# Norm chains with pre-added squares, one root table, and three output tiles abreast behind a norm

## The chip, the cores and the metric

The kernel runs on one core of one Trainium2 chip. The metric is device time in microseconds of one execution, as the median of several.

## The reference

Two layers of a diffusion backbone over 512 tokens (256 context, 256 latent), model width 1024, all in float32. What matters here:

```
def rmsnorm(x, g):
    y = xf * lax.rsqrt(jnp.mean(xf * xf, axis=-1, keepdims=True) + NORM_EPS)
    return y * g

for l in range(DEPTH):
    h  = modulate(rmsnorm(x, norm_mix_pre[l]), mod[0], mod[1])      # norm 0
    z  = h @ w_in[l]                                                # 24 tiles of 128 outputs
    ys = four mixers over z (short convolution, neighbourhood attention, GQA, RWKV-7)
    m  = merge_branches(h, ys, w_branch[l], w_gate[l], b_gate[l], w_o[l])
    x  = x + mod[2] * rmsnorm(m, norm_mix_post[l])                  # norm 1
    f  = conv_ffn(modulate(rmsnorm(x, norm_ffn_pre[l]), mod[3], mod[4]), ...)   # norm 2
    x  = x + mod[5] * rmsnorm(f, norm_ffn_post[l])                  # norm 3

def conv_ffn(h, w_up, w_conv, w_down):
    u = dwconv3(h @ w_up, w_conv)
    return (u[..., :D_FF] * jax.nn.silu(u[..., D_FF:])) @ w_down
```

In the second layer only the latent half is needed after the mixers, so most tiles there are 256 columns wide instead of 512.

## The kernel before

Features lie on partitions (1024 features are KT = 8 slices of 128), tokens on columns. Each weight column block of 128 outputs ("half" of a ring slot) gives one output tile. Matmuls of the projections are done in three products: ScalarE copies a weight half from `ring` to `whi` (rounded, L751), VectorE subtracts to get `wlo` (L1076), and `project` (L1502 to L1504) adds high by high, high by low and low by high for each of the 8 slices into one PSUM bank. There are SPLIT = 3 slots of `whi`/`wlo`; a slot is refilled when the tile that used it is done (`split_until`, on both engines). The ring has three slots of 1 MB, loaded by SyncE's queue (L577) in a fixed order; a slot is reloaded when both its halves are split, or for the modulation weights when TensorE has used it.

A norm goes through four engines. ScalarE squares each slice (`square`, L724); TensorE adds the squares over partitions and slices with eight matmuls against ones (`sum_squares`, L1483, full float32, two passes each); ScalarE makes the root as exp(-0.5 ln(mean + eps)) (`norm_root`, L730 and L733), each of the two functions behind a table load; VectorE multiplies. Norms 1 and 3 end in `residual` (L1137, L1143): slice by slice into X. Norms 0 and 2 end in a modulated input: VectorE times the root (L1129), ScalarE scale and shift (L779) and rounded copy (L785), VectorE the low part (L1115), one slice after the other, each counted in `h_ready`; the next projection waits slice by slice in its first tile alone (`made`).

Norm 1 reads the out-projection (`wo`), whose 8 tiles are copied to OB (L1012) and squared from there. Norm 3 does so with the down projection (F, L1051). Norm 3 also needs X back from DRAM: GpSimd's queue issues that load (L707) when the last down tile is done, because the feed-forward's hidden values lie over X. Then it issues the small bias tables of the next layer. At the end of layer 0 TensorE also makes three blocks of modulation values (L1518, L1525), from ring slots that the first z weights wait for.

In the up projection the bank of a tile is copied by ScalarE with a convolution factor (L1039), VectorE adds the two neighbours (L1440, L1442), in program order ahead of the next low half for the same pair of tiles. In the z projection banks are only copied.

Every engine executes its own program in order; semaphores join them. The order of TensorE's jobs is a list (`JOB`), each job takes the next of 8 banks.

Of the kernel before, what the change touches and what calls it, by code (L numbers as in the profile page):

```python
# [17 lines left out]
ALU = mybir.AluOpType  # L18
# [6 lines left out]
KT = DM // P  # L25
# [7 lines left out]
FT = DFF // P  # L33
# [48 lines left out]

STRIP = 32
STRIPS = P // STRIP
RING = 3
SLOT_N = 256
SPLIT = 3
NBANK = 8


# [184 lines left out]
def half_no(job):  # L275

    return HALF[blocks_of(job)[0]]


def build(nc, a, out):  # L280
    ctx = ExitStack()
    with ctx:
# [3 lines left out]
        def sem(name):  # L286
            return ctx.enter_context(nc.semaphore(name))
# [163 lines left out]
        u_lo = sem("u_lo")  # L451
        setup = sem("setup")
        sq_ready = sem("sq_ready")
        h_full = sem("h_full")
        scaled = sem("scaled")
        h_half = sem("h_half")
# [45 lines left out]
        def frees(name):  # L502

            return bank_free[JOB[name] % NBANK]

        def emptied(eng, name):

            eng.wait_ge(frees(name), JOB[name] // NBANK + 1)

# [10 lines left out]
        def norm_no(l, k):  # L520
            return 4 * l + k
# [193 lines left out]
        def _(act):  # L715
# [7 lines left out]
            def square(dst, src):  # L723
                act.activation(dst, src, ACT.Square).then_inc(sq_ready, 1)  # L724
# [73 lines left out]
            for l in range(LAYERS):  # L798
# [188 lines left out]
                for J in range(4):  # L987
# [17 lines left out]
                    for j in (2 * J, 2 * J + 1):  # L1005
                        act.wait_ge(gated, added(l, j, 3))
                        act.activation(AR[:, 0, j, c0:c1], ACC[:, j, c0:c1], ACT.Copy).then_inc(acc_hi, 1)

                for j in range(KT):
                    s = filled(act, ("wo", l, j))  # L1010
                    split_until(min(half_no(("wo", l, j)) + 1 + SPLIT, half_no(("up", l, 0, 0)) + SPLIT))
                    act.activation(OB[:, j, c0:c1], s[:, c0:c1], ACT.Copy).then_inc(frees(("wo", l, j)), 1)  # L1012
                    emptied(act, ("wo", l, j))
                    square(SQB[:, j, c0:c1], OB[:, j, c0:c1])
                norm_root(l, 1)
                for i in range(KT):
                    act.wait_ge(x_ready, 16 * l + i + 1)
# [10 lines left out]
                for j in range(FT):  # L1028
# [14 lines left out]
                    emptied(act, ("up", l, j, 1))  # L1043
                    act.activation(dst, dst, ACT.Silu).then_inc(silu_done, 1)
                product_hi(FT - 1)
                for j in range(KT):
                    split_until(half_no(("down", l, j)) + (5 if j < KT - 1 else 3))
                    s = filled(act, ("down", l, j))
                    if j < KT - 1:
                        split_until(half_no(("down", l, j)) + 6)  # L1050
                    act.activation(F[:, j, c0:c1], s[:, c0:c1], ACT.Copy).then_inc(frees(("down", l, j)), 1)  # L1051
                    emptied(act, ("down", l, j))
                    square(SQF[:, j, c0:c1], F[:, j, c0:c1])
                norm_root(l, 3)
                fill(("end", l, 0))

# [2 lines left out]
        def _(dve):  # L1059
# [95 lines left out]
            for l in range(LAYERS):  # L1155
# [243 lines left out]
                for J in range(4):  # L1399
                    for i in range(4):  # L1400
                        for j in (2 * J, 2 * J + 1):
                            split_until(min(half_no(("gate", l, j, i)) + SPLIT, half_no(("wo", l, 0)) + SPLIT))
                            no = 8 * J + 2 * i + (j - 2 * J)
                            gt = (rt, rs)[no % 2][:, c0:c1]
                            s = filled(dve, ("br", l, j, i))[:, c0:c1]
                            emptied(dve, ("gate", l, j, i))
                            o = ACC[:, j, c0:c1]
                            dst = o if i == 0 else gt
                            dve.tensor_tensor(dst, gt, s, ALU.mult).then_inc(frees(("br", l, j, i)), 1)  # L1409
                            emptied(dve, ("br", l, j, i))  # L1410
                            if i:
                                dve.tensor_tensor(o, o, gt, ALU.add).then_inc(gated, 1)
                        if READOUT.get((J, i)) == "g2":
                            readout()
                    for j in (2 * J, 2 * J + 1):
                        dve.wait_ge(acc_hi, 8 * l + j + 1)
                        dve.tensor_tensor(AR[:, 1, j, c0:c1], ACC[:, j, c0:c1], AR[:, 0, j, c0:c1].bitcast(F32),
                                          ALU.subtract).then_inc(acc_lo, 1)
                for j in range(KT):
                    split_until(min(half_no(("wo", l, j)) + 1 + SPLIT, half_no(("up", l, 0, 0)) + SPLIT))  # L1420

                gains(l, (1, 2, 3))
# [21 lines left out]
                    if j:  # L1444
                        product_lo(j - 1)
                product_lo(FT - 1)
                split_until(half_no(("down", l, 0)) + 3 * KT)
                for j in range(KT):
                    emptied(dve, ("down", l, j))
                dve.wait_ge(x_back, 32 * (l + 1))  # L1450
# [6 lines left out]
        def _(pe):  # L1457
# [10 lines left out]
            def done(ins):  # L1468
                count[0] += 1
                ins.then_inc(mm_done, 1)  # L1470
# [7 lines left out]
            def sum_squares(l, k, src):  # L1478
                c0, c1 = cols(l) if k else (0, T)
                o = job(("ss", l, k))  # L1480
                for i in range(KT):
                    pe.wait_ge(sq_ready, 8 * norm_no(l, k) + i + 1)
                    last = pe.matmul(o[:, c0:c1], K("ones"), src[:, i, c0:c1], start=(i == 0), stop=(i == KT - 1))  # L1483
                done(last)
# [8 lines left out]
            def project(name, part, c0, c1, kn=KT, made=None):  # L1493
# [14 lines left out]
                        last.then_inc(w_used, 1)  # L1508
                done(last)

            def fill(point):
                for name in FILL.get(point, []):
                    if name[0] == "mod":
                        w = weights(("ada",) + name[1:])
                        o = job(name)
                        for k in range(KT):
                            g = k % STRIPS
                            last = pe.matmul(o[STRIP * g:STRIP * g + STRIP, 0:SLOT_N], cpad[:, k, :], w[:, k, :],  # L1518
                                             start=(k < STRIPS), stop=(k >= KT - STRIPS))
                    else:  # L1520
                        pe.wait_ge(const_in, 16)
                        emptied(pe, ("mod",) + name[1:])
                        o = job(name)
                        for x in range(2):
                            last = pe.matmul(o[:, 2 * x:2 * x + 2], mrow[:, P * x:P * x + P], K("fold", 2),  # L1525
                                             start=True, stop=True)
                    done(last)

            pe.wait_ge(silu_c, 1)
            for l in range(LAYERS):  # L1530
                c0, c1 = cols(l)
                fill(("start", l, 0))
                sum_squares(l, 0, YB)
                fill(("start", l, 1))
                for n, t in enumerate(Z_ORDER):
                    z0, z1 = cols(l, t)
                    project(("z", l, t), lambda x, k: HR[:, x, k, z0:z1], z0, z1,
                            made=None if n else (h_ready, 16 * l))
                    if n == 5:
                        for i in range(3):  # L1540
                            q0, q1 = cols(l, Z_GQ + i)
# [285 lines left out]
                sum_squares(l, 1, SQB)  # L1827
                sum_squares(l, 2, SQB)

                for j in range(FT):  # L1830
                    for g in range(2):
                        project(("up", l, j, g), lambda x, k: H2[:, x, k, c0:c1], c0, c1,
                                made=None if j or g else (h_ready, 16 * l + 8))
                for j in range(KT):
                    project(("down", l, j), lambda x, k: hidden(x, k)[:, c0:c1], c0, c1, FT,
                            made=None if j else (u_lo, FT * l))
# [49 lines left out]
```

## Time and profile before

| | before |
|---|---|
| median of 3 runs | 2061.64 us (2061.12 to 2065.96) |
| the profiled execution | 2068.02 us, span 2066.2 us |
| TensorE busy | 1911.5 us, 93% |
| VectorE busy | 985.8 us, 48% |
| ScalarE busy | 821.6 us, 40% |
| GpSimd busy | 284.1 us, 14% |
| granted TensorE clock, mean | 0.962 |
| table loads on L730 and L733 | 8 and 8, 1283 ns each |

The span is the time from the first to the last instruction of one profiled execution; busy is the time in which an engine executed. An instruction's row names kernel line, engine, operation and tiles, out<-in. The clock is the share of TensorE's full clock (2.4 GHz) that was granted. Matmuls overlap, so their starts are compared, not their durations.

### The profile page before, as it was taken

Reading aid. Unit: us, or ns where it says so; the run is one execution under the profiler, and the core shown is the slowest. Engines: PE = TensorE matmul, PEld = TensorE weight load, DVE = VectorE, ACT = ScalarE, POOL = GpSimd, SP = SyncE. Lnnn points to the kernel's source line nnn. Section 1 sums busy time; section 2 is a strip of 40 time slices with the busy share of each in tenths; the row PEclk is TensorE's granted clock in tenths of the full one; section 3 lists DMA queues with packets and bytes.
Section 4 is the critical chain, followed back from the end, with each engine's and each line's share of the span. In section 5 each row is a group of like instructions: output and inputs, shape, how many; then the busy total and the mean of one; then the engine's idle time right before and its main releaser. Section 6 shows DMA issues by size and latency. Waiting matters only on the chain. (4 is left out here: it accounts for less than half of the span.)

```text
span 2066.2 us, 27988 instructions
## 1 busy us (share of the span) xinstructions
PE 1911.5 (93%) x11608; PEld 1571.5 (76%) x11608; DVE 985.8 (48%) x1555; ACT 821.6 (40%) x1306; POOL 284.1 (14%) x227
## 2 busy tenths in 40 slices
PE   4899998989999999799999996999897999989997
PEld 1688557959877777478888883875695989979997
DVE  1353437456333333455554215544646535557763
ACT  2421455152232223543433225325515234366653
POOL 1040432021000000011121001304202000002211
PEclk9899999989999999899999997999898999989999
DMA  8632642020342322223232336533101045444654
GB/s 243 212 101 82 194 145 82 1 76 7 88 157 82 102 68 96 82 67 117 82 102 78 96 112 174 188 119 119 62 1 62 1 133 166 159 135 150 198 160 126
DMA packets 225646, 228.64 MB, mean 111 GB/s; under 512 B 5169, under 2 KB 214321, under 8 KB 225393
## 3 DMA queue, kind: packets, MB, share of 16 engines
q1 hardware_dynamic: 210560, 190.40, 29.2%
q0 software_dynamic: 14960, 36.44, 6.1%
q8 instruction: 94, 1.54, 0.3%
q14 instruction: 32, 0.25, 0.0%
HBM read 214.24 MB, written 12.58 MB: 110 GB/s over the span
## 5 line engine op out<-in xcount | busy, mean ns | idle before, releaser
L751 ACT ACTIVATE whi<-ring 128x1024 fp32r<-128x1024 f32 (+1 forms) x264 | 275.4, 1046 | 688.4 <-PE ps L1504 624.8
L1076 DVE TENSOR_TENSOR wlo<-ring,whi 128x1024 fp32r<-128x1024 f32 (+1 forms) x264 | 319.4, 1213 | 212.8 <-ACT whi L751 212.1
L1502 PE MATMUL ps<-H,whi 128*128 128x512 f32 (+1 forms) x704 | 241.0, 342 | 13.1 <-DVE H L1115 13.0
L1503 PE MATMUL ps<-H,whi 128*128 128x512 f32 (+1 forms) x704 | 238.9, 339 | 0.0
L1504 PE MATMUL ps<-H,wlo 128*128 128x512 f32 (+1 forms) x704 | 238.7, 339 | 0.0
L1502 PE MATMUL ps<-HG,whi 128*128 128x512 f32 (+1 forms) x512 | 181.3, 354 | 0.1
L1504 PE MATMUL ps<-HG,wlo 128*128 128x512 f32 (+1 forms) x512 | 172.1, 336 | 0.0
L1503 PE MATMUL ps<-HG,whi 128*128 128x512 f32 (+1 forms) x512 | 172.1, 336 | 0.0
L1502 PE MATMUL ps<-HR,whi 128*128 128x512 f32 (+1 forms) x384 | 144.3, 376 | 23.1 <-DVE HR L1115 23.1
L1502 PEld LDWEIGHTS ps<-H,whi 128*128 128x128 f32 x704 | 134.7, 191 | 32.0 <-issue 13.4
L1504 PEld LDWEIGHTS ps<-H,wlo 128*128 128x128 f32 x704 | 135.1, 192 | 13.8
L1503 PEld LDWEIGHTS ps<-H,whi 128*128 128x128 f32 x704 | 135.2, 192 | 13.5
L1503 PE MATMUL ps<-HR,whi 128*128 128x512 f32 (+1 forms) x384 | 140.9, 367 | 0.0
L1504 PE MATMUL ps<-HR,wlo 128*128 128x512 f32 (+1 forms) x384 | 140.8, 367 | 0.0
L1502 PEld LDWEIGHTS ps<-HG,whi 128*128 128x128 f32 x512 | 97.1, 190 | 14.3 <-issue 4.5
L1502 PE MATMUL ps<-UA,whi 128*128 128x512 f32 (+1 forms) x320 | 107.5, 336 | 0.0
L1503 PE MATMUL ps<-UA,whi 128*128 128x512 f32 (+1 forms) x320 | 107.5, 336 | 0.0
L1504 PE MATMUL ps<-UA,wlo 128*128 128x512 f32 (+1 forms) x320 | 107.5, 336 | 0.0
L1503 PEld LDWEIGHTS ps<-HG,whi 128*128 128x128 f32 x512 | 97.1, 190 | 13.6 <-issue 3.8
L1504 PEld LDWEIGHTS ps<-HG,wlo 128*128 128x128 f32 x512 | 97.1, 190 | 10.1
L1502 PEld LDWEIGHTS ps<-HR,whi 128*128 128x128 f32 x384 | 74.6, 194 | 39.4 <-issue 19.5
L1409 DVE TENSOR_TENSOR rt<-rt,ps 128x512 f32<-128x512 f32 (+1 forms) x24 | 13.3, 554 | 160.1 <-PE ps L1809 152.8
(285 smaller groups left out, 3619.1 us busy)
## 6 DMA issues: line engine op xcount, KB each, us to landing
ring<-in_ada_w SPq DMA_DIRECT2D x48, 1024.0 KB, 5.3
ring<-in_ffn_up SPq DMA_DIRECT2D x44, 1024.0 KB, 5.1
ring<-in_w_gate SPq DMA_DIRECT2D x32, 1024.0 KB, 5.5
ring<-in_w_in SPq DMA_DIRECT2D x24, 1024.0 KB, 5.2
ring<-in_ffn_down SPq DMA_DIRECT2D x32, 512.0 KB, 3.9
WB<-in_w_branch POOLq DMA_DIRECT2D x8, 1024.0 KB, 7.3
ring<-in_w_o SPq DMA_DIRECT2D x8, 1024.0 KB, 5.3
ring<-in_ffn_down SPq DMA_DIRECT2D x16, 384.0 KB, 3.5
```

The costliest lines, as they stand in the source:

```text
L751: act.activation(whi[:, m % SPLIT, 0:kn, :], ring[:, SLOT[raw] % RING, 0:kn, P * half:P * half + P], ACT.Copy).then_inc(hi_done, 1)
L1076: dve.tensor_tensor(wlo[:, m % SPLIT, 0:kn, :], ring[:, SLOT[raw] % RING, 0:kn, P * half:P * half + P], whi[:, m % SPLIT, 0:kn, :].bitcast ...
L1409: dve.tensor_tensor(dst, gt, s, ALU.mult).then_inc(frees(("br", l, j, i)), 1)
L1502: pe.matmul(o[:, c0:c1], hi[:, i, :], part(0, k), start=(k == 0), stop=False)
L1503: pe.matmul(o[:, c0:c1], hi[:, i, :], part(1, k), start=False, stop=False)
L1504: last = pe.matmul(o[:, c0:c1], lo[:, i, :], part(0, k), start=False, stop=(k == kn - 1))
```

## The change

Four edits:

- Squares of norms 1 and 3 are taken from the PSUM bank ahead of the copy. VectorE adds squares 1 to 6 to square 0 as they come (`sum_square`), in the loops over `wo` and `down`; `sum_squares` then makes two matmuls, over slice 0 (the sum of seven) and slice 7. For norms 0 and 2 it keeps its eight.
- The last weight half behind the out-projection is split after the square and the copy instead of before.
- `preload_act_table_set("natural_log_exp_and_others")` stands ahead of the `wo` loop and of the `down` loop.
- `project_first` replaces `project` for the first three tiles of z and of up: slices 0 to 4 go through all three tiles, then each tile takes its last three slices.

```diff
+ROOT_TABLE = "natural_log_exp_and_others"
+ABREAST = 5
...
+                act.preload_act_table_set(ROOT_TABLE)
                 for j in range(KT):
                     s = filled(act, ("wo", l, j))
-                    split_until(min(half_no(("wo", l, j)) + 1 + SPLIT, half_no(("up", l, 0, 0)) + SPLIT))
+                    if j < KT - 1:
+                        split_until(min(half_no(("wo", l, j)) + 1 + SPLIT, half_no(("up", l, 0, 0)) + SPLIT))
+                    square(SQB[:, j, c0:c1], s[:, c0:c1])
                     act.activation(OB[:, j, c0:c1], s[:, c0:c1], ACT.Copy).then_inc(frees(("wo", l, j)), 1)
-                    emptied(act, ("wo", l, j))
-                    square(SQB[:, j, c0:c1], OB[:, j, c0:c1])
+                split_until(half_no(("up", l, 0, 0)) + SPLIT)
                 norm_root(l, 1)
...
+                act.preload_act_table_set(ROOT_TABLE)
                 for j in range(KT):
                     split_until(half_no(("down", l, j)) + (5 if j < KT - 1 else 3))
                     s = filled(act, ("down", l, j))
                     if j < KT - 1:
                         split_until(half_no(("down", l, j)) + 6)
+                    square(SQF[:, j, c0:c1], s[:, c0:c1])
                     act.activation(F[:, j, c0:c1], s[:, c0:c1], ACT.Copy).then_inc(frees(("down", l, j)), 1)
-                    emptied(act, ("down", l, j))
-                    square(SQF[:, j, c0:c1], F[:, j, c0:c1])
                 norm_root(l, 3)
...
+                def sum_square(k, SQ, j):
+                    n = 2 * l + k // 2
+                    dve.wait_ge(sq_ready, 8 * norm_no(l, k) + j + 1)
+                    if j > 1:
+                        dve.wait_ge(sq_summed, (KT - 2) * n + j - 1)
+                    dve.tensor_tensor(SQ[:, 0, c0:c1], SQ[:, 0, c0:c1], SQ[:, j, c0:c1], ALU.add).then_inc(sq_summed, 1)
                 for j in range(KT):
+                    if 1 < j:
+                        sum_square(1, SQB, j - 1)
                     split_until(min(half_no(("wo", l, j)) + 1 + SPLIT, half_no(("up", l, 0, 0)) + SPLIT))
...
-                split_until(half_no(("down", l, 0)) + 3 * KT)
+                for j in range(KT):
+                    split_until(half_no(("down", l, 0)) + min(3 * j + 6, 3 * KT))
+                    if 0 < j < KT - 1:
+                        sum_square(3, SQF, j)
...
             def sum_squares(l, k, src):
-                for i in range(KT):
+                if k % 2:
+                    pe.wait_ge(sq_summed, (KT - 2) * (2 * l + k // 2 + 1))
+                for i in (0, KT - 1) if k % 2 else range(KT):
                     pe.wait_ge(sq_ready, 8 * norm_no(l, k) + i + 1)
                     last = pe.matmul(o[:, c0:c1], K("ones"), src[:, i, c0:c1], start=(i == 0), stop=(i == KT - 1))
...
+            def project_first(names, part, cs, made):
+                outs = [job(name, n) for n, name in enumerate(names)]
+                tiles = []
+                for name in names:
+                    tiles += halves(name)
+                order = [(k, n) for k in range(ABREAST) for n in range(len(names))]
+                order += [(k, n) for n in range(len(names)) for k in range(ABREAST, KT)]
+                for k, n in order:
+                    c0, c1 = cs[n]
+                    o, (hi, lo) = outs[n][:, c0:c1], tiles[n]
+                    if n == 0:
+                        pe.wait_ge(made[0], made[1] + k + 1)
+                    pe.matmul(o, hi[:, k, :], part(0, k)[:, c0:c1], start=(k == 0), stop=False)
+                    pe.matmul(o, hi[:, k, :], part(1, k)[:, c0:c1], start=False, stop=False)
+                    last = pe.matmul(o, lo[:, k, :], part(0, k)[:, c0:c1], start=False, stop=(k == KT - 1))
+                    if k == KT - 1:
+                        done(last)
...
+                project_first([("z", l, t) for t in Z_ORDER[:SPLIT]], lambda x, k: HR[:, x, k, :],
+                              [cols(l, t) for t in Z_ORDER[:SPLIT]], (h_ready, 16 * l))
...
+                ups = [("up", l, j, g) for j in range(FT) for g in range(2)]
+                project_first(ups[:SPLIT], lambda x, k: H2[:, x, k, :], [(c0, c1)] * SPLIT, (h_ready, 16 * l + 8))
+                for name in ups[SPLIT:]:
+                    project(name, lambda x, k: H2[:, x, k, c0:c1], c0, c1)
```

## Rows read from the trace of the kernel before

**Rows 1.** Timeline, all engines, layer 0, norm 1: start us, duration, instruction, [idle <-releaser]
```profile
843.56 7.03 PE L1483 MATMUL ps<-SQB,con 128*128 128x512 f32 x16
843.84 1.06 ACT L751 ACTIVATE whi<-ring 128x1024 fp32r<-128x1024 f32 x1 [3.23 <-PE ps L1504]
...
845.41 0.63 ACT L724 ACTIVATE SQB<-OB 128x512 f32<-128x512 f32 x1
...
846.26 0.17 DVE L1102 TENSOR_TENSOR amod<-mod,vec 128x16 f32<-128x16 f32 x1
...
851.33 1.28 ACT L733 ACT_TABLE_LOAD   x1
...
853.39 1.29 DVE L1137 TENSOR_TENSOR OB<-OB,rs 128x512 f32<-128x512 f32 x2 [6.96 <-ACT rs L733]
```

**Rows 2.** The same timeline at norm 2 of layer 0
```profile
866.60 0.69 ACT L730 ACTIVATE rt<-ps,eps 128x512 f32<-128x512 f32 x1
```

**Rows 3.** Timeline, layer 0, up projection: first tile, second tile, fourth weight's low half
```profile
873.58 0.77 PE L1502 MATMUL ps<-H,whi 128*128 128x512 f32 x1 [7.05 <-DVE H L1115]
...
884.02 0.39 PE L1502 MATMUL ps<-H,whi 128*128 128x512 f32 x1
```
```profile
887.42 1.22 DVE L1076 TENSOR_TENSOR wlo<-ring,whi 128x1024 fp32r<-128x1024 f32 x1
```

**Rows 4.** Timeline, layer 0, z projection: first matmul of the first and fourth tile
```profile
66.99 0.76 PE L1502 MATMUL ps<-HR,whi 128*128 128x512 f32 x1 [5.28 <-DVE HR L1115]
```
```profile
88.11 0.39 PE L1502 MATMUL ps<-HR,whi 128*128 128x512 f32 x1
```

**Rows 5.** Timeline from the last down tile of layer 0 to norm 0 of layer 1
```profile
1238.11 0.92 POOL L707 DMA_DIRECT2D X<-xsave  x1 [114.83 <-PE ps L1504]
...
1245.73 60.31 SPq L577 DMA_DIRECT2D ring<-in_w_in  x7
...
1248.01 1.29 DVE L1137 TENSOR_TENSOR F<-F,rs 128x512 f32<-128x512 f32 x2 [23.21 <-DMA X<-xsave]
...
1259.29 0.63 ACT L724 ACTIVATE YB<-X 128x512 f32<-128x512 f32 x1 [0.16 <-DVE X L1143]
...
1269.84 1.90 DVE L1129 TENSOR_TENSOR Z<-X,rs 128x512 f32<-128x512 f32 x3 [2.71 <-ACT rs L733]
```

**Rows 6.** Timeline, TensorE, layer 1, z projection
```profile
1274.09 0.55 PE L1502 MATMUL ps<-HR,whi 128*128 128x256 f32 x1 [12.93 <-DVE HR L1115]
...
1284.49 0.41 PE L1502 MATMUL ps<-HR,whi 128*128 128x256 f32 x1
...
1288.91 0.28 PE L1502 MATMUL ps<-HR,whi 128*128 128x256 f32 x1
...
1294.74 0.39 PE L1502 MATMUL ps<-HR,whi 128*128 128x512 f32 x1
```

**Rows 7.** Timeline, layer 1, norm 1 and the up projection
```profile
1835.37 1.06 ACT L751 ACTIVATE whi<-ring 128x1024 fp32r<-128x1024 f32 x1 [1.10 <-PE ps L1504]
```
```profile
1841.08 0.76 DVE L1137 TENSOR_TENSOR OB<-OB,rs 128x256 f32<-128x256 f32 x2 [3.11 <-ACT rs L733]
...
1863.49 1.22 DVE L1076 TENSOR_TENSOR wlo<-ring,whi 128x1024 fp32r<-128x1024 f32 x1
```
```profile
1854.24 0.55 PE L1502 MATMUL ps<-H,whi 128*128 128x256 f32 x1 [4.86 <-DVE H L1115]
...
1860.80 0.41 PE L1502 MATMUL ps<-H,whi 128*128 128x256 f32 x1
...
1867.21 0.28 PE L1502 MATMUL ps<-H,whi 128*128 128x256 f32 x1
```

**Rows 8.** Timeline, VectorE, norm 3 of layer 1
```profile
2055.58 0.76 DVE L1137 TENSOR_TENSOR F<-F,rs 128x256 f32<-128x256 f32 x2 [12.39 <-DMA X<-xsave]
```

**Rows 9.** Windows: busy time of each engine, granted clock, DMA share, GB/s
```profile
66.90:70.20 3.30, 3.21 (x7) 2.15 (x8) 1.39 (x2) 3.30 (x8) 0.00 (x0) 0.50 0.83 292
```
```profile
1606.00:1650.00 44.00, 44.00 (x387) 43.69 (x386) 28.85 (x43) 9.57 (x18) 0.00 (x0) 1.00 0.01 1
```

More of the change, by code:

```diff
@@ L453, in build @@
         sq_ready = sem("sq_ready")
+        sq_summed = sem("sq_summed")
         h_full = sem("h_full")
@@ L1534, in _ @@
                 fill(("start", l, 1))
+                project_first([("z", l, t) for t in Z_ORDER[:SPLIT]], lambda x, k: HR[:, x, k, :],
+                              [cols(l, t) for t in Z_ORDER[:SPLIT]], (h_ready, 16 * l))
                 for n, t in enumerate(Z_ORDER):
                     z0, z1 = cols(l, t)
-                    project(("z", l, t), lambda x, k: HR[:, x, k, z0:z1], z0, z1,
-                            made=None if n else (h_ready, 16 * l))
+                    if n >= SPLIT:
+                        project(("z", l, t), lambda x, k: HR[:, x, k, z0:z1], z0, z1)
                     if n == 5:
@@ L1828, in _ @@
                 sum_squares(l, 2, SQB)
[L1830 to L1833, printed above, removed]
+                ups = [("up", l, j, g) for j in range(FT) for g in range(2)]
+                project_first(ups[:SPLIT], lambda x, k: H2[:, x, k, :], [(c0, c1)] * SPLIT, (h_ready, 16 * l + 8))
+                for name in ups[SPLIT:]:
+                    project(name, lambda x, k: H2[:, x, k, c0:c1], c0, c1)
                 for j in range(KT):
```

## The prediction

> **What bounds the kernel now.** TensorE is busy for 93% of the span, so the first question is where it waits. I read the timeline at the places where a norm feeds a projection. The first matmul of each such projection carries its wait: 7.05 us before the up projection of layer 0 [rows 3], 12.93 us before the z projection of layer 1 [rows 6], 4.86 us before the up projection of layer 1 [rows 7]. In front of these waits TensorE sums squares at the pace of other engines. Then the timeline of all engines through one norm [rows 1] gives the chain inside. Then the timeline at the end of each layer, where a norm root has a rival for the latest arrival, the reload of X [rows 5, 8]. Everything else in the projections is paced by TensorE and the change leaves it so.
>
> I call three matmuls of one slice (high by high, high by low, low by high) a triple, and the eight triples of a tile its work. In layer 1's z projection seven triples at 256 columns took 1288.91 - 1284.49 = 4.42 us, or 0.64 each, with matmuls of 0.41 us; from 1288.91 the same matmul lasts 0.28, and one narrow triple with the eight at 512 columns behind it took 1294.74 - 1288.91 = 5.83 us [rows 6], which is 0.36 + 8 x 0.68. The granted clock has two levels: 0.50 (1.2 GHz) in a stretch of layer 0's z, 1.00 (2.4 GHz) in the mixing stage [rows 9], and the step at 1288.9 is that between them. So a triple takes 0.36 and 0.68 us at full clock for the two widths, 0.64 and, twice that, 1.28 at half.
>
> **Norm 1, layer 0.** Before, ScalarE sees the last out-projection tile at 843.84, splits a weight half (1.06), copies the bank, squares (0.63), and waits: TensorE needs 7.03 us for the eight column sums, which begin at 843.56 and end at 850.6. Then logarithm (0.69, [rows 2]), table load 1.28, exponential, and the residual starts at 853.39 [rows 1]. After, six of the eight sums are made on VectorE. Each is an addition of 128x512, which I price by the two multiplications of that shape, 1.29 us [rows 1]; VectorE has one 1.22 us split [rows 3] in each tile of the out-projection (8 x 0.68 = 5.4 us), so the six lie hidden. In layer 1 they cost about 0.4 each beside 1.2 in 2.9 us; hidden too. Without that cover they would cost 6 x 0.65 = 3.9 us in layer 0. TensorE does two sums: the first at once, the second when the last square is there (844.5), 7.03 / 8 = 0.88 us, ready at 845.5. ScalarE now does square 0.6, copy 0.6, split 1.06, to 846.1, then logarithm 0.7 and exponential 0.6 with no load: root at 847.4. What is late next is VectorE: its low half of the split starts when ScalarE has split, and the gain products follow. Before, the last of these ended at 846.43, 1.5 us after the split's 844.90 [rows 1]; after, 846.1 + 1.5 = 847.6, and with the semaphores between some 847.9. Gain 853.39 - 847.9 = 5.5 us.
>
> **Norm 2, layer 0.** The first load hides already: squares end, TensorE still sums, the logarithm starts at 866.60 without a wait behind its load [rows 2], one 1.28 us load after a last square that needed about as long on TensorE. Only the second load goes: 1.3 us.
>
> **The price of a load.** In the rows a load lasts 1.28 us, from 851.33 to 852.61, and the residual starts at 853.39 [rows 1]; of the 0.78 us between, some 0.63 are the exponential (the square of that shape takes as long). The Trainium skill, ScalarE: Activation LUTs, section What ACT_TABLE_LOAD costs, gives 1.28 us for the load and 1.38 us for a drain beside it; with six exposed loads gone (below) the sum would be 6 x 1.38 = 8.3 us better by it. The trace disagrees: 0.15 us are left for a drain.
>
> **Norm 1 and 2, layer 1.** The same with 256 columns: from 1835.37 square 0.4, copy 0.4, split 1.06, then 1.5 to the end of the gains and 0.2 for semaphores, so 1838.9 instead of 1841.08 [rows 7]: 2.2 us. Norm 2: 1.3 us.
>
> **Norm 3, both layers: nothing.** The residual waits for X, not for the root: in layer 0 VectorE's wait of 23.21 us ends with the DMA of X at 1248.01, issued when the last down tile was done, 1238.11 [rows 5]; in layer 1 the same, 12.39 us to 2055.58 [rows 8]. The shorter chain ends earlier behind a transfer that doesn't move. The load put ahead of the down loop costs 1.28 us of ScalarE, while TensorE has a split half in hand. I price it at nothing; uncovered it would be 1.3 us a layer.
>
> **Norm 0 of layer 1: where a collision starts.** Before: X lands at 1247.9, last square at 1259.9, a wait for weights, three splits, load, logarithm, load, exponential, and the first product at 1269.84 [rows 5]. After, both loads go (norm 3 left the right table, and only squares and copies run between). But TensorE is free 5 us sooner after the last down tile, its modulation matmuls release ring slots, and the first w_in load, issued at 1245.73 [rows 5], is issued near 1240.7: inside the 9.7 us of the X load. If they share the rate, X lands about 3 us later, 1251. From X's landing: 12.0 to the last square (as before), three splits 3.1, logarithm and exponential 1.3: X + 16.5 = 1267.8 against 1269.84. Gain 2.0 us. If X isn't delayed, 5.4; if it lands at 1256, a loss of 2.7.
>
> **Three tiles abreast.** The first tile of z in layer 1 took 1284.49 - 1274.09 = 10.4 us for eight slices of the normed input [rows 6], so a slice of 512 columns comes about every 1.5 us (the last two come closer), and one triple takes 0.68. After, each slice up to the fifth feeds three triples, 2.0 us, so TensorE doesn't wait for input once it has begun. The work is the same, so what counts is when the third tile ends, and the clock.
> z, layer 0: from 66.99 to 88.11, where the fourth begins, 21.1 us [rows 4]. The window 66.9 to 70.2 has clock 0.50 [rows 9]. After: 3.3 us at half clock (2.6 triples), 21.4 triples x 0.68 = 14.6, so 17.9. Gain 3.2, rounded with the start to 3.3.
> up, layer 0: the first tile from 873.58 to 884.02 [rows 3], two more of 5.45, 21.3 us. After: 5.4 us at half clock (as in z of layer 1, below; 4.2 triples) plus 19.8 x 0.68 = 18.9. Then a new wait. All three split slots are held until the first tile ends, which is now two threes of triples (4.1 us) ahead of the third's end, not two tiles. Before, from that tile's end (884.02) the low half of the fourth weight started at 887.42 and took 1.22: 4.6 us [rows 3], behind a bank evacuation and two convolution steps. So a wait of 0.6 us. Gain 2.4 - 0.6 = 1.8.
> z, layer 1: 1274.09 to 1294.74, 20.65 us, at half clock to 1288.9 [rows 6]. After: tiles of 256, 256 and 512 columns, a slice is 2.56 us at half clock and 1.40 at full. 5.4 us at half clock (an estimate: the second tile starts without a gap at 1284.49 and the step comes 4.4 us later [rows 6], with a triple or two ahead of it), the rest of five slices to 9.45, then 0.36 x 3 + 0.36 x 3 + 0.68 x 3: 13.65. Gain 7.0. The fourth weight is late by nothing: z has no convolution before its split.
> up, layer 1: 1854.24 to 1867.21, 12.97 us [rows 7]. After, the three tiles would end at 11.0, but the fourth weight comes 3.9 us after the first tile's end (before 1860.80 to 1863.49 plus 1.22), that is at 8.9 + 3.9 = 12.8. Gain 0.1; between -0.9 and 1.1 with the clock's rise at 7.9 or 3.3 us.
> Sum: norms 5.5 + 1.3 + 2.2 + 1.3 + 2.0 = 12.3; abreast 3.3 + 1.8 + 7.0 + 0.1 = 12.2; together 24.5 us.
>
> The profiled execution took 2068.02 us with a span of 2066.2, so I expect a span near 2041.7; its time is 6.4 us over the median of 2061.64. I take the 24.5 from the median: **2037 us**, 1.2% less.
>
> **The rivals.**
> 1. The clock stays low while three banks alternate. The Trainium skill, TensorE: Matmul & The Clock Gate, section A second HAM failure mode: psum-queue depth-cycling, says that cycling through banks lets the clock fall back. As a mechanism of this kernel: z and up of layer 0 wholly at half clock, 24 x 1.28 = 30.7 us instead of 21.1 and 21.3; z of layer 1 20.5, even; up of layer 1 24 x 0.64 = 15.4 instead of 13.0. Together 21.3 us lost against 12.3 gained: 9 us slower, 2070.6. It decides once some 49 us more are at half clock (each costs half of itself, and 24.5 must go). Against it: between 1606 and 1650 TensorE goes to another bank every four matmuls, for 44 us, at a granted clock of 1.00 [rows 9].
> 2. The weight splits pace the restart everywhere: the late fourth weight, which I have at 0.6 and 1.8 us in the up projections, eats all 12.2 us. For it: the 4.6 us of [rows 3]. Against: z has a shorter way. 2061.64 - 12.3 = 2049.
> 3. The loads stay in front of logarithm and exponential. Norm 1 and 2 of layer 0 lose 2.3 + 1.3, of layer 1 1.9 + 1.3, norm 0 of layer 1 2.6: 9.4 us less, 2046.5. The trace of before has no load that serves both functions.
> 4. The early w_in loads hold X back to 1256: 4.7 us less, 2042.
>
> **How the numbers follow.** Forecast 0.72; rival 1 0.04, rival 2 0.10, rival 3 0.05, rival 4 0.07, the rest unnamed. The forecast's own bounds: X undelayed +3.4, no stall at up 0.6 + 1.8 + clock 1 a place give about 2029; X at 1256 and the late clock rises give 2044. The range reaches past rival 3 and stops short of rival 2: 2029 to 2047. A change under 0.3% (6 us) couldn't be told from none here. Faster 0.93, same 0.04, slower 0.03.
>
> **What would show it.** In the new trace: no table load between logarithm and exponential of norms 1 to 3; two column sums after the last out-projection tile and the residual of layer 0 some 4 us after its end instead of 9.5; residuals of norm 3 still waiting for X; the landing of X in layer 0, 9.7 us after issue or 13; the first three z tiles of layer 1 in 13.7 us; a wait of 0.6 and 1.8 us before the fourth up tile. The prediction is wrong if TensorE's clock stays at 0.5 in the abreast stretches, if those waits are several us, or if X comes so late that the norm of layer 1 gains nothing.

## The result, and the profile after

The changed kernel takes **2040.14 us** (median of 4 runs, 2039.36 to 2044.38); the kernel before took 2062.61 us beside it. The ratio is 0.9893, 95% interval 0.9874 to 0.9912: 22 us less, where 24.5 were forecast. The profiled span is 2037.5 us; 2041.7 was forecast.

From the page of the changed kernel: the row of its part 1 with each engine's busy time, the clock's row of its part 2, and two of its groups (line, operation, busy us, mean ns, idle before and releaser):

```profile
PE 1884.8 (93%) x11560; PEld 1557.2 (76%) x11560; DVE 996.3 (49%) x1579; ACT 803.5 (39%) x1296; POOL 284.2 (14%) x227
...
PEclk9899998989999999899999997999898999989998
...
L1081 DVE TENSOR_TENSOR wlo<-ring,whi 128x1024 fp32r<-128x1024 f32 (+1 forms) x264 | 319.3, 1212 | 198.9 <-ACT whi L754 198.2
L1522 PE MATMUL ps<-H,whi 128*128 128x512 f32 (+1 forms) x656 | 220.7, 336 | 2.3 <-DVE wlo L1081 2.2
```

TensorE is still busy for 93%; it has 27 us less of busy time, since twenty-four column sums are gone and fewer projection matmuls run at half clock. The second group's 2.3 us of idle are new: the two waits for the fourth weight. Everything else must be read place by place. I cut both traces at the same instructions, and took the time from one cut to the next. The norm stages behind a projection begin where the first column sum starts, which is the end of the last tile. "First product" is VectorE's first multiplication by the root:

| stage, us | before | after | change | forecast |
|---|---|---|---|---|
| z layer 0, first to fourth tile | 21.12 | 18.01 | -3.1 | -3.3 |
| norm 1 layer 0, last out-projection tile to residual | 9.83 | 3.80 | -6.0 | -5.5 |
| residual to first product of norm 2 | 15.94 | 14.63 | -1.3 | -1.3 |
| up layer 0, first to fourth tile | 21.34 | 19.92 | -1.4 | -1.8 |
| last down tile to residual (norm 3) | 10.37 | 10.96 | +0.6 | +3 |
| residual to first product of norm 0, layer 1 | 21.83 | 19.41 | -2.4 | -5 |
| z layer 1 | 20.65 | 13.39 | -7.3 | -7.0 |
| norm 1 layer 1 | 5.99 | 3.20 | -2.8 | -2.2 |
| norm 2 layer 1 | 10.64 | 8.84 | -1.8 | -1.3 |
| up layer 1 | 12.97 | 12.92 | -0.1 | -0.1 |
| mixing, layer 0 and layer 1 | 755.45, 540.35 | 755.39, 537.92 | -2.5 | 0 |

The stages that the change touches give 25.6 us and the mixing stages and the start 3.4 more; the stretches of the feed-forward between the cuts took 0.3 longer, which leaves the 28.7 between the two spans. The medians differ by less, 22.5, so part of the 28.7 must be scatter; the experiments show where it comes from.

**Norm 1 of layer 0**, the timeline of all engines (start, duration, instruction, idle before it), to be held against [rows 1]:

```profile
839.47 1.97 PE L1503 MATMUL ps<-SQB,con 128*128 128x512 f32 x4
839.67 0.60 ACT L727 ACTIVATE SQB<-ps 128x512 f32<-128x512 f32 x1 [3.33 <-PE ps L1524]
840.16 0.59 ACT L1018 ACTIVATE OB<-ps 128x512 f32<-128x512 f32 x1
...
840.64 1.06 ACT L754 ACTIVATE whi<-ring 128x1024 fp32r<-128x1024 f32 x1
841.59 0.69 ACT L733 ACTIVATE rt<-ps,eps 128x512 f32<-128x512 f32 x1
841.73 1.23 DVE L1081 TENSOR_TENSOR wlo<-ring,whi 128x1024 fp32r<-128x1024 f32 x1 [4.50 <-ACT whi L754]
842.31 0.63 ACT L736 ACTIVATE rs<-rt 128x512 f32<-128x512 f32 x1
...
843.06 0.17 DVE L1107 TENSOR_TENSOR amod<-mod,vec 128x16 f32<-128x16 f32 x1
843.27 1.29 DVE L1142 TENSOR_TENSOR OB<-OB,rs 128x512 f32<-128x512 f32 x2
```

TensorE has two sums instead of eight, ScalarE goes from split to logarithm to exponential with no load, and the residual has no wait in brackets: VectorE's own low half (to 842.96) and the gains, not the root (842.94), are last, as forecast. Of 16 loads on the two root lines 2 are left, both in norm 0 of layer 0 (36.3 and 43.6 us). The two preloads bring 4 new ones, which stand ahead of the loops and show in none of the norm stages.

**The end of layer 0** has the timeline rows and the DMA issues (KB each, median us to landing) that answer to [rows 5]. The last two fences are from the kernel before and weren't shown yet: its w_in loads, and ScalarE's two waits for them:

```profile
1225.35 0.92 POOL L710 DMA_DIRECT2D X<-xsave  x1 [114.83 <-PE ps L1524]
1226.27 5.30 POOL L600 DMA_DIRECT2D bm<-in_na_bias  x8
...
1227.93 15.33 SPq L580 DMA_DIRECT2D ring<-in_w_in  x3
...
1235.85 1.29 DVE L1142 TENSOR_TENSOR F<-F,rs 128x512 f32<-128x512 f32 x2 [23.20 <-DMA X<-xsave]
```
```profile
1247.12 0.63 ACT L727 ACTIVATE YB<-X 128x512 f32<-128x512 f32 x1 [0.16 <-DVE X L1148]
1250.22 2.00 ACT L754 ACTIVATE whi<-ring 128x1024 fp32r<-128x1024 f32 x2 [2.47 <-DMA ring<-in_w_in]
1252.93 1.06 ACT L754 ACTIVATE whi<-ring 128x1024 fp32r<-128x1024 f32 x1 [0.71 <-DMA ring<-in_w_in]
```
```profile
ring<-in_w_in SPq DMA_DIRECT2D x4, 1024.0 KB, 23.2
X<-xsave POOLq DMA_DIRECT2D x1, 2048.0 KB, 10.3
```
```profile
ring<-in_w_in SPq DMA_DIRECT2D x4, 1024.0 KB, 17.2
```
```profile
1261.94 2.00 ACT L751 ACTIVATE whi<-ring 128x1024 fp32r<-128x1024 f32 x2 [2.02 <-DMA ring<-in_w_in]
1264.81 1.06 ACT L751 ACTIVATE whi<-ring 128x1024 fp32r<-128x1024 f32 x1 [0.86 <-DMA ring<-in_w_in]
```

The first w_in load is issued 3.0 us after the last down tile instead of 8.1. X hardly notices (10.3 us against 9.7). But w_in gains nothing either: its loads take 23.2 us instead of 17.2, and ScalarE, done with the squares at 1247.75, stands 2.47 + 0.71 us waiting for them, where it stood 2.02 + 0.86 before. So the stage lost its two loads, 2.57 us, and nothing of its wait for weights.

**The projections.** TensorE's timeline at the first and fourth z tile of layer 1, then the windows (length; busy us of PE, PEld, DVE, ACT, POOL; granted clock; DMA share; GB/s) on both sides of the clock's rise; to be held against [rows 6]:

```profile
1259.51 0.55 PE L1545 MATMUL ps<-HR,whi 128*128 128x256 f32 x1 [10.51 <-DVE HR L1120]
...
1272.90 0.39 PE L1522 MATMUL ps<-HR,whi 128*128 128x512 f32 x1
```
```profile
1259.60:1264.60 5.00, 5.00 (x19) 4.53 (x20) 4.25 (x7) 5.00 (x12) 0.00 (x0) 0.55 0.00 0
1264.60:1272.90 8.30, 8.30 (x56) 7.53 (x54) 6.65 (x9) 5.88 (x11) 2.69 (x3) 1.00 0.34 83
```

TensorE is busy for every microsecond of both windows, and 4.6 us after its start the clock is at 2.4 GHz although each triple goes to another bank than the last. In the other three abreast stretches it rises after 3.4 (z, layer 0), 6.0 (up, layer 0) and 5.4 us (up, layer 1). The fourth up tile, first of layer 0, then of layer 1, against [rows 3] and [rows 7]:

```profile
882.07 0.47 PE L1522 MATMUL ps<-H,whi 128*128 128x512 f32 x1 [0.52 <-DVE wlo L1081]
...
1838.31 0.36 PE L1522 MATMUL ps<-H,whi 128*128 128x256 f32 x1 [1.70 <-DVE wlo L1081]
```

These are the forecast waits, 0.6 and 1.8 us.

### The profile page after: what moved, and what is told of

It is laid out like the page before. It is cut to its first block and busy times, and to the rows that moved or that the text cites. A ratio compares the mean times of both kernels' runs of the same rounds, so it can differ in the third digit from the quotient of the medians.

```text
span 2037.5 us, 27926 instructions
## 1 busy us (share of the span) xinstructions
PE 1884.8 (93%) x11560; PEld 1557.2 (76%) x11560; DVE 996.3 (49%) x1579; ACT 803.5 (39%) x1296; POOL 284.2 (14%) x227
## 5 line engine op out<-in xcount | busy, mean ns | idle before, releaser
L1522 PE MATMUL ps<-H,whi 128*128 128x512 f32 (+1 forms) x656 | 220.7, 336 | 2.3 <-DVE wlo L1081 2.2
L1523 PE MATMUL ps<-H,whi 128*128 128x512 f32 (+1 forms) x656 | 220.4, 336 | 0.0
L1524 PE MATMUL ps<-H,wlo 128*128 128x512 f32 (+1 forms) x656 | 220.4, 336 | 0.0
L1522 PEld LDWEIGHTS ps<-H,whi 128*128 128x128 f32 x656 | 124.5, 190 | 15.9 <-issue 3.0
L1523 PEld LDWEIGHTS ps<-H,whi 128*128 128x128 f32 x656 | 124.5, 190 | 12.8
L1524 PEld LDWEIGHTS ps<-H,wlo 128*128 128x128 f32 x656 | 124.5, 190 | 12.6
L1522 PE MATMUL ps<-HR,whi 128*128 128x512 f32 (+1 forms) x336 | 122.8, 365 | 0.0
L1523 PE MATMUL ps<-HR,whi 128*128 128x512 f32 (+1 forms) x336 | 121.5, 361 | 0.0
L1524 PE MATMUL ps<-HR,wlo 128*128 128x512 f32 (+1 forms) x336 | 121.4, 361 | 0.0
L1523 PEld LDWEIGHTS ps<-HG,whi 128*128 128x128 f32 x512 | 97.1, 190 | 13.7 <-issue 3.8
L957 ACT ACTIVATE Z<-ps 128x512 f32<-128x512 f32 x64 | 33.0, 603 | 140.3 <-PE ps L1717 140.3
```

What stands on the lines that cost most here:

```text
L957: act.activation(TT[:, h, :, :], s, ACT.Copy).then_inc(frees(("tt", l, d, z, h)), 1)
L1522: pe.matmul(o[:, c0:c1], hi[:, i, :], part(0, k), start=(k == 0), stop=False)
L1523: pe.matmul(o[:, c0:c1], hi[:, i, :], part(1, k), start=False, stop=False)
L1524: last = pe.matmul(o[:, c0:c1], lo[:, i, :], part(0, k), start=False, stop=(k == kn - 1))
```

## The experiments

Two theories stood at the start. A: the change is the sum of the forecast steps, each at its place, and what lies between is scatter. B: something general came with it, in the mixing stages or through the clock.

**The kernel before, unchanged.** 

> The kernel before, unchanged, for a second profile. Theory A: the 28.7 us between the two spans hold some 5 us that are the scatter of one execution (the profiled execution of before took 2068, its median is near 2062), among them the 2.4 us by which the stage from the fourth z tile of layer 1 to the end of its out-projection was shorter, and the 0.9 us before the first z tile; then this profile shows a span near 2061 and that stage within 0.5 us of 537.9. Rival B: the change shortened that stage; then it is again 540.3 us here. Ratio 1.000 within 0.002.

Measured 2065.83 us (12 runs), ratio 0.9995 (0.9983 to 1.0007). Its mixing stages took 758.15 and 536.08 us, where the first profile had 755.45 and 540.35. So one kernel's mixing stages move by 2.7 and 4.3 us, and the 4.3 us of layer 1 are more than the 2.43 us that I had to explain. Nothing in the mixing stages asks for B; whether part of it holds through the clock is taken up under "Where the scatter sits". The repeat also gives the scatter of the other stages. Norm 0 of layer 1 took 20.64 us in it (21.83 in the first profile), z of layer 1 19.66 (20.65) and norm 2 of layer 1 10.44 (10.64); the other rows of the table stayed within 0.2 us.

**The chain alone**, without three tiles abreast.

```diff
-                project_first(ups[:SPLIT], ...)
-                for name in ups[SPLIT:]:
-                    project(name, lambda x, k: H2[:, x, k, c0:c1], c0, c1)
+                        project(("up", l, j, g), lambda x, k: H2[:, x, k, c0:c1], c0, c1,
+                                made=None if j or g else (h_ready, 16 * l + 8))
```

(and the same for z)

> Squares summed on VectorE, banks squared first and the root table, without the three tiles abreast. Theory A (each place gains by itself): norm 1 of layer 0 6.0, norm 2 1.3, layer 1 2.8 and 1.8, norm 0 of layer 1 1.8, together 13.7 us less than before, 2048.9. Rival B (the abreast tiles and the chains share one gain, the earlier rise of the clock): over 16 us, under 2046.

2056.64 us, ratio 0.9950 (0.9936 to 0.9965): 10 us, 7 to 13, so the 13.7 of theory A lie just outside the interval, and rival B's 16 far outside. The norm stages show all of the chain's gain: norm 1 3.79 and 3.21 us, norm 2 14.64 and 8.98, norm 3 with norm 0 2.75 less, 14.5 us together. The abreast stretches are as before (21.12, 21.30, 20.64, 13.35). In this profile the mixing stages took 3.1 us more than in the first profile of before, and the feed-forward of layer 1 1.5 us more.

**Abreast alone**: the kernel before with `project_first`.

> Three tiles abreast alone, the norms as before. Theory A: z of layer 0 3.1, up 1.4, z of layer 1 7.3, up 0.05, together 11.9 us less, 2050.7, with waits of 0.5 and 1.7 us before the fourth up tiles. Rival B (shared gain): under 9 us, above 2053.5.

2054.62 us, ratio 0.9938 (0.9923 to 0.9953): 13 us, 9.5 to 16. z and up take 18.92, 19.80, 14.09 and 11.82, 11.4 us less than before where 11.9 were expected. The waits before the fourth up tiles are 0.52 and 1.70 us, as expected. The norms take what they took before (norm 2 of layer 1 0.4 us less than in the repeat). The two halves give 23.1 us apart and 22.1 together: they add up, within intervals of 3 us on either side of each.

**The root table alone**: the kernel before with the two preloads.

```diff
+                act.preload_act_table_set(ROOT_TABLE)
                 for j in range(KT):
                     s = filled(act, ("wo", l, j))
```

> The kernel before with only the two preloads of the root table. Theory A: one load of 1.28 us goes from the chain at norms 1 and 2 of both layers and two at norm 0 of layer 1, six in all, 7.7 us, 2054.9. Rival B (a load costs a drain of 1.38 us beside it, as the Trainium skill has it, ScalarE: Activation LUTs, What ACT_TABLE_LOAD costs): 6 x 2.66 = 16 us, 2046.6. Rival C (the wait for weights at norm 0 of layer 1 takes the two loads back): 5.1 us, 2057.5.

2056.01 us, ratio 0.9949 (0.9935 to 0.9962), 10.5 us. Norm 1 goes from 9.83 to 8.54 and from 5.99 to 4.70. ScalarE's timeline there, where [rows 1] had two loads:

```profile
853.15 0.69 ACT L731 ACTIVATE rt<-ps,eps 128x512 f32<-128x512 f32 x1 [4.58 <-PE ps L1486]
853.87 0.63 ACT L734 ACTIVATE rs<-rt 128x512 f32<-128x512 f32 x1
```

One exposed load is worth 1.29 us at each of these places, its own 1.28 and nothing of a drain. The Trainium skill, ScalarE: Activation LUTs, section What ACT_TABLE_LOAD costs, would have 2.66; this run disagrees with its drain of 1.38 us. Taken first, the load is 1.29 of the 6.03 us of norm 1; the other 4.74 came with the fewer column sums and the later split. The split depends on which edit is taken first; the other order wasn't run. The run gained some 3 us more than theory A expected (the interval is 8 to 13 us). Norm 0 took 18.36 us, 3.5 or 2.3 less than in the two profiles of before, where two loads are worth 2.6. Norm 2 of layer 1 took 8.24, 2.4 or 2.2 less instead of 1.3; what shortened it beyond the load wasn't looked for.

**All eight slices abreast**, `ABREAST = 8`: the slots of the splits come free only at the end of the third tile.

> The changed kernel with all eight slices abreast instead of five, so the three split slots come free together at the end of the third tile. Theory A (what is late behind the abreast tiles is the fourth weight, some 2.8 us after the first tile's end in z, 4.6 and 3.9 us in up of layers 0 and 1): first to fourth tile 19.4 us in z of layer 0 (18.0 with five), 22.6 in up (19.9), 15.1 in z of layer 1 (13.4), 14.4 in up (12.9), together 7.3 us slower than with five. Rival B (the weights are early enough, the order doesn't matter): the same four times within 0.5 us.

2052.20 us, ratio 0.9931 (0.9907 to 0.9956), some 8 us worse than with five (0.9893; each ratio from its own comparison). The four stretches take 20.82, 22.69, 14.91 and 14.38 us, 8.6 us more than with five, where 7.3 were expected. Theory A holds, with z of layer 0 1.4 us over its figure; the clock was low for 5.6 us of it instead of 3.4. TensorE's waits (us in total, times, longest) say why:

```profile
PE ps L1522 <- DVE wlo L1081: 10.0, 5, 3.2
```

With five slices it was 2.2 us in 2 waits. So rival 2 of the prediction names a real mechanism, which the five slices mostly avoid.

**The bias tables of the next layer early.** GpSimd's queue issued them right behind the load of X, in front of w_in's arrival.

```diff
-                if l == 1:
-                    emptied(pool, ("g2", 0, 1))
-                    load_small(1)
...
                 pool.dma_start(xsave[:, c0:c1]..., X[:, :, c0:c1]).then_inc(x_saved, 16)
+                if l == 0:
+                    emptied(pool, ("g2", 0, 1))
+                    load_small(1)
```

> The changed kernel, with the bias tables of layer 1 (eight loads of small packets) issued by GpSimd behind the save of X in layer 0 instead of behind the reload of X. Theory A (these loads hold the w_in loads back, which landed about 25 us after the last down tile however early they were issued): the first two w_in loads land before the squares are done, the stage from the residual of norm 3 to norm 0's first product takes 16.5 us instead of 19.4, and 2.9 us go. Rival B (the bytes of X and w_in alone fill the DMA engines): 19.4 us as before, no change.

Residual to first product went from 19.41 to 16.36 us, and the issues of the same stretch read:

```profile
ring<-in_w_in SPq DMA_DIRECT2D x4, 1024.0 KB, 11.9
X<-xsave POOLq DMA_DIRECT2D x1, 2048.0 KB, 11.0
```

23.2 us from issue to landing became 11.9, with w_in's bytes the same. Theory A of the run holds: what held w_in back was the bias loads, not X. ScalarE's wait for w_in is gone. How much that wait is worth scatters: it was 3.18 us in the first profile of the change, 2.82 in its repeat and 1.27 in the run with the fourth up weight split first, which doesn't touch this place, and the stage took 19.41, 19.05 and 17.50 us. It took 16.36 in all three runs with the early bias tables. Norm 3 in front of it took 11.66 us instead of 10.96, so the two stages together gained 2.4 us here. The whole kernel took 2042.80 us, ratio 0.9880 (0.9851 to 0.9909), no measurable gain over the change.

**Half of X reloaded.** The FFN's hidden values lie over slices 0 to 3 alone, so the others need not come back.

```diff
-                pool.dma_start(X[:, :, c0:c1], xsave[:, c0:c1]...).then_inc(x_back, 16)
+                pool.dma_start(X[:, 0:4, c0:c1], xsave[0:4 * P, c0:c1]...).then_inc(x_back, 16)
```

> The changed kernel, reloading only slices 0 to 3 of X (the hidden values lie over these alone). Theory A (norm 3's residual waits for X and for nothing else): from the last down tile to the residual 6.5 us instead of 11.0 in layer 0 and 4.3 instead of 6.6 in layer 1; the end of the kernel 2.3 us sooner, while in layer 0 most is given back at the wait for w_in. Together 3 to 5 us less. Rival B (the latency of the DMA, not its size, sets the wait): under 1 us in each layer.

2040.01 us, ratio 0.9867 (0.9842 to 0.9893). The residual starts 6.93 us after the last down tile instead of 10.96, in layer 1 4.57 instead of 6.62. That is near the 6.5 and 4.3 of theory A, and far from rival B. In layer 0 some of the 4.0 us are given back at the next wait, ScalarE's for w_in; norm 0 took 20.64 us, 1.2 more than in the first profile of the change and 1.6 more than in its repeat:

```profile
1250.38 2.00 ACT L754 ACTIVATE whi<-ring 128x1024 fp32r<-128x1024 f32 x2 [3.70 <-DMA ring<-in_w_in]
```

**The fourth up weight split first**, ahead of VectorE's convolution steps for the first pair.

```diff
+                        ahead = 0 if j or g else 1
-                        split_until(min(half_no(("up", l, j, g)) + SPLIT, half_no(("down", l, 0)) + SPLIT))
+                        split_until(min(half_no(("up", l, j, g)) + SPLIT + ahead, half_no(("down", l, 0)) + SPLIT))
```

> The changed kernel, with VectorE's low half of the fourth up weight ahead of the first tile's two convolution steps. Theory A (these steps make the wait before the fourth tile): the waits of 0.5 and 1.7 us before the fourth up tile vanish; first to fourth tile 19.4 us in layer 0 (19.9) and 11.3 in layer 1 (12.9), 2.1 us less. Rival B (ScalarE's high half comes too late by itself): at least 1 us of wait stays in layer 1.

The fourth tile of layer 1 now waits 0.42 us instead of 1.70, and that of layer 0 no more:

```profile
1840.98 0.36 PE L1523 MATMUL ps<-H,whi 128*128 128x256 f32 x1 [0.42 <-DVE wlo L1081]
```

So theory A holds nearly, and rival B doesn't. A later up tile of layer 1 waits 0.99 us for its low half at 1882.59 us. Up of layer 1 goes from 12.92 to 11.67 us. Up of layer 0 takes 17.78 us, 0.7 less than the 18.45 of the change's repeat below, which had the same low spell of the clock. The whole takes 2043.01 us, ratio 0.9885 (0.9863 to 0.9906).

**The change again, and with the edits together.** All three, the change unchanged, and the change with the reload and bias edits, side by side:

> The changed kernel with the three edits of the earlier runs together: bias tables of layer 1 issued behind the park of X, only slices 0 to 3 of X reloaded at the residual behind the FFN, and the fourth up tile split ahead of VectorE's backlog. Theory A (the rests found after the change are separate: w_in transfers held back by the bias loads, the residual waiting for all of X, the split behind the tile switch): the gains add up. Against the changed kernel: norm 0 of layer 1 from 19.4 to about 16.5 us and this time the earlier residual (6.9 against 11.0 us) isn't given back in layer 0, since w_in lands early: together 7 us; norm 3 of layer 1 2.1 us, up 1.3 (layer 1) and 2.1 (layer 0). In sum 12 us, some of it given back in the mixing stages: span near 2026, ratio to the kernel before about 0.983. Rival B (norm 0 has a floor that none of the three moves, VectorE's own chain of sums, roots and products behind the residual): the stages norm 3 and norm 0 in layer 0 together stay at 27.5 us or more (6.9 plus 20.6), as with the half reload alone, and the ratio stays at 0.986 or above.

> The changed kernel once more, unchanged, as the base of this comparison. Theory A (the changed kernel's stages repeat, only the mixing stages scatter by some 5 us from one execution to the next): norm, up and first z stages within 0.5 us of those of its first profile (18.0, 3.8, 19.9, 11.0 + 19.4, 13.4, 3.2 us), ratio to the kernel before 0.989 within 0.0015. Rival B (the stages themselves scatter): one of them moves by over 1 us.

> The changed kernel with the early bias tables and the half reload of X together, without the change to the up split. Theory A (the half reload was given back in layer 0 only since ScalarE stood waiting for w_in): norm 3 6.9 us and norm 0 at 16.5 us in layer 0, 4.4 us less than with the early bias tables alone; with 2.1 us in layer 1 the ratio is about 0.985. Rival B (it was given back since VectorE's work behind the residual sets norm 0, whatever w_in does): norm 3 6.9 and norm 0 19 to 21 us, so the ratio stays at 0.987 to 0.988.

| | median us | ratio to before | norm 3 + norm 0 | up, layer 0 and 1 |
|---|---|---|---|---|
| the change again | 2040.52 | 0.9876 (0.9857 to 0.9896) | 10.92 + 19.05 | 18.45, 12.91 |
| reload and bias | 2031.92 | 0.9837 (0.9819 to 0.9855) | 6.67 + 16.37 | 19.85, 12.93 |
| all three | 2035.26 | 0.9853 (0.9834 to 0.9871) | 6.72 + 16.36 | 19.16, 11.70 |

Theory A of the two combinations holds for norm 3 and norm 0: alone, the half reload left 6.93 + 20.64, with the bias tables moved it keeps both gains, 7 us in layer 0. The ratio of all three, 0.9853, missed the 0.983 of its theory A, and it isn't the 0.986 or above of rival B either. That of reload and bias is 0.9837, where about 0.985 was expected. The w_in loads take less time still, and ScalarE's wait for them is gone:

```profile
ring<-in_w_in SPq DMA_DIRECT2D x4, 1024.0 KB, 8.8
X<-xsave POOLq DMA_DIRECT2D x1, 1024.0 KB, 6.0
```

"Reload and bias" is the best version measured, 8.6 us below the change in the same comparison. The third edit saves 1.2 us in the up stage of layer 1 and 0.7 in that of layer 0, yet the median with it is 3.3 us higher; the intervals overlap, so it can't be called a gain or a loss.

**Where the scatter sits.** The change again, by my own expectation, should have kept up of layer 0 at 19.9, and had 18.45: its rival B is right there, by the bound of 1 us that I had set. The difference lies in the granted clock. Windows over the same 10 us of that stage, first profile of the change, then its repeat:

```profile
862.00:872.00 10.00, 9.85 (x31) 7.93 (x32) 7.76 (x13) 8.83 (x18) 0.00 (x0) 0.69 0.02 5
```
```profile
865.70:875.70 10.00, 10.00 (x38) 8.15 (x39) 7.58 (x12) 8.65 (x18) 0.00 (x0) 0.86 0.01 2
```

0.69 is 6.2 us at 1.2 GHz, 0.86 is 2.8 us, and half of the difference is 1.7 us of time, where the stages differ by 1.5. The mixing stages go the same way. Two stretches in layer 1, in the kernel before and in its repeat:

```profile
1440.00:1490.00 50.00, 39.62 (x236) 29.67 (x237) 33.70 (x53) 34.14 (x56) 13.74 (x12) 0.80 0.21 67
...
1560.00:1620.00 60.00, 48.98 (x341) 38.21 (x341) 39.03 (x65) 37.01 (x61) 15.20 (x14) 0.86 0.17 53
```
```profile
1440.00:1490.00 50.00, 39.05 (x260) 30.00 (x261) 36.07 (x56) 34.32 (x57) 13.84 (x13) 0.86 0.21 66
1560.00:1620.00 60.00, 49.14 (x350) 39.16 (x349) 41.40 (x66) 37.22 (x61) 15.18 (x14) 0.89 0.17 53
```

With the clock's own records, summed over each mixing stage of all 13 profiles: in layer 0, 27.3 us at 1.2 GHz go with 755.4 to 755.6 us (once 758.2), 30.7 with 758.2 to 758.5, 34.1 with 759.6. In layer 1, 27.3 go with 536.1 to 537.9, 30.7 with 539.1, 34.1 with 540.6, 37.5 with 540.4 to 542.0. The 12 runs of the repeat agree: the two fastest, 2060.45 and 2060.91 us, have a mean clock of 0.966, the three slowest, 2068.33 to 2072.36, one of 0.959 to 0.961. So the differences between stages where no work was changed go with how long the clock stayed low in them. No run sets the clock, so this is read from profiles side by side. Layer 1's 37.5 us came up in the first profile of before, in the chain alone and in all five versions with a bias, reload or up edit, and not in the two profiles of the change. Whether an edit upstream brings it about, and with it 4 to 5 us back, these profiles can't say; it would be why the bias edit alone, 2 to 2.4 us faster in norm 3 and norm 0 together, measured no faster. That stays open.

## Why the prediction was right

By its own steps:

- **Norm 1.** Forecast 5.5 and 2.2 us, measured 6.03 and 2.79. The mechanism was right to the last releaser, VectorE's split and gains. The size was short by 0.5. I had 1.2 us for square and copy, and they took 0.97 from 839.67 to 840.64, since one starts before the other ends. I had 0.3 for semaphores, and the residual starts 0.04 after the last gain (843.23 to 843.27).
- **The price of a load.** 1.28 us forecast, 1.29 measured where one exposed load alone was removed.
- **Norm 2.** 1.3 forecast in each layer; 1.31 and 1.80. In layer 1 the repeat of before leaves 1.6; what the 0.3 to 0.5 beyond the load are stays open.
- **Norm 3: nothing.** The residual still ends a wait for X, of 23.20 and, in layer 1, 12.09 us.
- **Norm 0 of layer 1.** Forecast: X lands 3 us later, the first product 5.3 us sooner behind it, 2.0 in sum. Measured 0.6 later and 2.4 sooner, 1.8 in sum. This step was right only as a sum, and that is luck: two errors of 2.5 and some 3 us cancelled. The early w_in loads were issued when I had them (3.0 us after the last down tile, 3.1 forecast), but didn't take X's rate; they were slowed themselves. And "From X's landing: 12.0 to the last square (as before), three splits 3.1, logarithm and exponential 1.3" leaves out the wait for weights that the same paragraph names in the kernel before. It was 2.89 us there, and it stayed, 3.18 us. With it gone (the bias edit) the stage took 16.36 us; 16.5 was forecast.
- **Three abreast.** 3.3, 1.8, 7.0 and 0.1 forecast; 3.1, 1.4, 7.3 and 0.1 measured. The new waits came as forecast, 0.52 and 1.70 us. The gains depend on the clock: up in layer 0 gained 1.4 us with 6.0 us low, 2.9 in the repeat with 2.8. Z in layer 1 gained 7.3 us against the first profile of before and 6.3 against its repeat.
- **Rival 1**, the clock stays low while banks alternate: it rose after 3.4 to 6.0 us in all four stretches, and stood at 1.00 for the rest of z in layer 1. The Trainium skill, TensorE: Matmul & The Clock Gate, section A second HAM failure mode: psum-queue depth-cycling, tells of a kernel that cycles through banks and has short idle moments between its groups of matmuls, whose clock falls and rises again. Three banks in turn didn't bring it here, with TensorE busy for 5.00 of 5.00 and 8.30 of 8.30 us in z of layer 1; a stretch with such idle moments wasn't tried.
- **Rival 2** takes nearly all of the gain in layer 1's up stage, as forecast, and nothing in z. With eight slices it takes more in all four stretches.
- **Rival 3**, the loads stay: 2 of 16 are left.
- **Rival 4**, X at 1256 of the old time: X landed 0.6 us later.
- **The base.** I took 24.5 us from the median; the touched stages gave 25.6, and 22.5 stood between the medians, within the interval of the ratio (18 to 26 us).

## What to carry to other kernels

Where a norm feeds a projection, cut the trace at both ends of the chain and price each link by its own row; the links of norm 1 added up to within 0.6 us here. When an engine or a load is moved forward, list all waits that its successor has, not only the one that ended last: one dropped wait for weights held back 1.3 to 3.2 us here, and a half reload alone gave a part back to it. Before calling a remainder of a few us an effect, compare how long the clock was low in the stages that weren't changed.

## What the hardware showed beside that

The eight bias loads, 96 KB each, cost more than their bytes. The queues' rows for the same 34 us of the change and of the bias edit (packets, MB, share of the 16 engines' time):

```profile
q0 software_dynamic: 912, 2.88, 39.0%
q1 hardware_dynamic: 3375, 3.41, 32.1%
```
```profile
q1 hardware_dynamic: 3579, 3.62, 32.8%
q0 software_dynamic: 528, 2.10, 19.8%
```

Without them GpSimd's queue has 0.78 MB and 384 packets less, and 19.2% of 34 us less, 6.5 us of all 16 engines: 120 GB/s. X on the same queue took 6.7 us for 2.10 MB, 313 GB/s, and w_in, in shorter packets, 10.9 us for 3.41 MB, 313 too. Why the bias packets are 2.6 times as dear per byte wasn't tried. Nor are the 6.5 us the whole of it: w_in landed 11.3 us sooner without these loads. And a table load behind which no drain shows, and a clock whose low spells in unchanged stages vary from one execution to the next by up to 10 us, are told above.
